# Attention scores as three products of split queries and keys, from one set of buffers

## The reference, cut to what matters

```python
q = (c_q @ w_uq).reshape(B, S, N_HEADS, QK_NOPE_DIM + QK_ROPE_DIM)
q_nope = q[..., :QK_NOPE_DIM]
q_rope = apply_rope(q[..., QK_NOPE_DIM:], cos[:, :, None, :], sin[:, :, None, :])
kv = (c_kv @ w_ukv).reshape(B, S, N_HEADS, QK_NOPE_DIM + V_HEAD_DIM)
k_nope, v = kv[..., :QK_NOPE_DIM], kv[..., QK_NOPE_DIM:]
for qs in range(0, S, Q_BLOCK):            # Q_BLOCK = 128
    qe = qs + Q_BLOCK
    s = (einsum('bqhd,bkhd->bhqk', q_nope[:, qs:qe], k_nope[:, :qe])
         + einsum('bqhr,bkr->bhqk', q_rope[:, qs:qe], k_rope[:, :qe])) * scale
    causal = arange(qe)[None, :] <= arange(qs, qe)[:, None]
    p = softmax(where(causal, s, -inf), axis=-1)
    outs.append(einsum('bqhk,bkhd->bqhd', p, v[:, :qe]))
```

## Time and profile before

| | us |
|---|---|
| median of 3 runs | 3156.41 (3155.97 to 3156.82) |
| the profiled execution | 3158.01, its span 3156.2 |
| PE busy over the whole span | 2728.8 (86%) |
| attention, from its first product to its last DVE write | 1432.2 to 1800.2 |

### The profile page before, as it was taken

One profiled execution on the slowest core, in us unless ns is written; L12 is line 12 of the kernel. 1 busy time (PEld: TensorE's weight loads), 2 busy tenths in 40 slices (PEclk: granted clock), 3 DMA queues, 4 the chain that ended last, 5 costly groups with the idle time before them and its releaser, 6 DMA issues. The chain is left out here.

```text
span 3156.2 us, 42227 instructions
## 1 busy us (share of the span) xinstructions
PE 2728.8 (86%) x16267; PEld 1769.1 (56%) x16269; DVE 1512.5 (48%) x2421; ACT 962.5 (30%) x1707; POOL 313.3 (10%) x378
## 2 busy tenths in 40 slices
PE   6999888979999999989999895897887758988785
PEld 3778687758888878755555583332322642333221
DVE  4248886577777757834555554111111760111114
ACT  6212275453333344434344321010110630110004
POOL 0000075000000000211011000111110000111100
PEclk9999999989999999999999996899999868999998
DMA  8511043122332266520000317999999669999996
GB/s 325 195 54 33 22 167 149 57 67 90 107 115 103 91 229 228 166 92 11 7 4 4 114 51 304 422 409 424 425 423 397 233 250 420 400 424 424 425 419 265
DMA packets 198828, 674.24 MB, mean 214 GB/s; under 512 B 42256, under 2 KB 83671, under 8 KB 144863
## 3 DMA queue, kind: packets, MB, share of 16 engines
q1 hardware_dynamic: 180192, 637.92, 51.8%
q0 software_dynamic: 18432, 33.60, 2.8%
HBM read 624.82 MB, written 80.15 MB: 223 GB/s over the span
## 5 line engine op out<-in xcount | busy, mean ns | idle before, releaser
L3335 PE MATMUL psum<-moe_ring,hreg 128*32 128x512 f32 x2832 | 481.5, 629 | 38.9 <-DMA moe_top<-in_moe_w 20.9
L3440 DVE TENSOR_TENSOR ex_hb<-ex_sil,psum 128x256 f32<-128x256 f32 x64 | 27.0, 421 | 567.4 <-ACT ex_sil L3413 567.4
L3335 PE MATMUL psum<-x,hreg 128*32 128x512 f32 x848 | 231.2, 662 | 56.4 <-DMA moe_ring<-in_moe_w 34.1
L3335 PEld LDWEIGHTS psum<-moe_ring,hreg 128*32 128x32 f32 x2832 | 140.9, 116 | 242.9 <-issue 197.1
L1507 PE MATMUL psum<-gu_hi,x1r 128*128 128x512 f32 x712 | 226.4, 394 | 9.4 <-DVE x1r L1634 5.1
L1860 PE MATMUL psum<-dn_op 128*128 128x512 f32 x924 | 211.7, 392 | 4.3 <-DVE dn_op L1955 4.3
L3387 PE MATMUL psum<-moe_ring,hreg 128*32 128x512 f32 x1216 | 196.8, 607 | 18.0 <-issue 10.9
L1860 PEld LDWEIGHTS psum<-dn_op 128*128 128x128 f32 x924 | 174.5, 189 | 41.5 <-DVE dn_op L1955 5.1
L3335 PE MATMUL psum<-moe_top,hreg 128*32 128x512 f32 x416 | 195.3, 625 | 0.0
L3413 ACT ACTIVATE ex_sil<-psum 128x256 f32<-128x256 f32 x64 | 24.5, 384 | 557.5 <-PE psum L3335 557.5
L1507 PE MATMUL psum<-gu_hi,gu_er 128*128 128x512 f32 x504 | 158.6, 389 | 0.0
(11 more groups left out here) (643 smaller groups left out, 5759.2 us busy)
## 6 DMA issues: line engine op xcount, KB each, us to landing
moe_ring<-in_moe_w SPq DMA_DIRECT2D x244, 1024.0 KB, 22.2
x<-in_moe_w SPq DMA_DIRECT2D x84, 1024.0 KB, 20.4
moe_top<-in_moe_w SPq DMA_DIRECT2D x48, 1024.0 KB, 26.7
x<-in_w_down SPq DMA_DIRECT2D x77, 256.0 KB, 2.9
x<-midrow SPq DMA_DIRECT2D x77, 256.0 KB, 3.5
XF<-in_w_ada SPq DMA_DIRECT2D x19, 1024.0 KB, 6.7
moe_ring<-yrow SPq DMA_DIRECT2D x16, 1024.0 KB, 11.3
xrow<-x SPq DMA_DIRECT2D x24, 512.0 KB, 3.7
```

The source lines that it names most:

```text
L3335: last = pe.matmul(ps[i][r, :], xT[i][:, k, r], place[HOME[n, j]][:, kk * 512:(kk + 1) * 512], start=k == 0, stop=k == KD - 1)
L3440: dve.tensor_tensor(hb[i][:, :], sil[q % 2][:, :], ps[i][:, DE:2 * DE], ALU.mult).then_inc(hbd, 1)
```

## The change

The scores are computed from queries and keys that are each split into a high part (rounded to fp32r) and a low part (the rest). Each float32 product becomes three fp32r products: high times high, high times low, low times high.

Queries go through one float32 buffer, `whole`, written by DVE from PSUM; ACT copies it to QH[w], DVE subtracts to get QL[w]. Keys of one head are copied by ACT from PSUM to KH[w], and DVE subtracts PSUM minus KH into KL[w]. The other head's keys wait in a float32 buffer, `second`, until their place is free; then ACT copies them to KH and DVE subtracts. There is one set of QH, QL, KH, KL, with a place for each head w, where QT and KT were there twice. So the order of items is by head: the head w = p % 2 first for t = 7 to 4, then the other head for t = 7 to 4 and 3 to 0, then the first again for t = 3 to 0. The k turn of pair p+1 stands behind item 11, the q turn of its first head behind item 12, the q turn of its second head behind item 0 of pair p+1 itself.

The core of the diff:

```diff
-PAIR_ITEMS = [(g, t, w) for g in (1, 0) for t in (4 * g + 3, 4 * g + 2, 4 * g + 1, 4 * g) for w in range(2)]
+def pair_items(p):
+    first = p % 2
+    return [(g, t, w) for g, heads in ((1, (first, 1 - first)), (0, (1 - first, first)))
+            for w in heads for t in (4 * g + 3, 4 * g + 2, 4 * g + 1, 4 * g)]
...
-            if p + 1 < HEAD_PAIRS and i in (8, 10, 12):
...
+            if p + 1 < HEAD_PAIRS and i == 11:
+                turns.append(("k", p + 1, 0))
+            if p + 1 < HEAD_PAIRS and i == 12:
+                turns.append(("q", p + 1, (p + 1) % 2))
+            if p > 0 and i == 0:
+                turns.append(("q", p, 1 - p % 2))
...
# PE
                     elif kind == "k":
                         pe.wait_ge(k_ev, p + 1)
+                        pe.wait_ge(k_lo, p + 1)
                     else:
-                        pe.wait_ge(q_ev, 2 * p + i + 1)
+                        pe.wait_ge(q_full, query_number(p, i) + 1)
...
+                    if i == 0:
+                        (waits for k_hi, k_lo, q_hi, q_lo of the first head)
+                    if i == 4:
+                        (waits for k2_hi, k2_lo, q_hi, q_lo of the second head)
...
                     if c:
-                        pe.matmul(S[:, 0:c], q, key[:, 0:c], start=True, stop=True)
-
-                    pe.matmul(S[:, c:e], q, key[:, c:e], start=True, stop=False)
+                        for x, y, z in ((QH, KH, 0), (QH, KL, 1), (QL, KH, 2)):
+                            pe.matmul(S[:, 0:c], x[w][:, rows], y[w][:, 0:c], start=z == 0, stop=z == 2)
+                    for x, y, z in ((QH, KH, 0), (QH, KL, 1), (QL, KH, 2)):
+                        pe.matmul(S[:, c:e], x[w][:, rows], y[w][:, c:e], start=z == 0, stop=False)
...
# ACT
+                    act.activation(KH[w][ROWS[w], :], bank(n)[ROWS[w], :], ACT.Identity, bias=0.0).then_inc(k_hi, 1)
+                    if p >= 1:
+                        act.wait_ge(k2_lo, p)
+                    act.activation(second[ROWS[1 - w], :], bank(n)[ROWS[1 - w], :], ACT.Identity, bias=0.0).then_inc(k_ev, 1)
+
+                def second_keys(n, p):
+                    w = 1 - p % 2
+                    act.wait_ge(item, n + 1)
+                    act.wait_ge(k_ev, p + 1)
+                    act.activation(KH[w][ROWS[w], :], second[ROWS[w], :], ACT.Identity, bias=0.0).then_inc(k2_hi, 1)
+
+                def queries(n, p, w):
+                    act.wait_ge(q_full, query_number(p, w) + 1)
+                    act.activation(QH[w][:, :], whole[:, :], ACT.Copy).then_inc(q_hi, 1)
...
+                for w in range(2):
+                    last = act.activation(KH[w][ROWS[1 - w], :], K.KT[0][w][ROWS[1 - w], :], ACT.Copy)
+                last.then_inc(rope_hi, 1)
...
# DVE
                 def queries(n, p, w):
                     dve.wait_ge(item, n + 1)
-                    dve.tensor_tensor(QT[p % 2][w][:, :], bank(n), K.CS[w][:, :], ALU.mult).then_inc(q_ev, 1)
+                    dve.wait_ge(q_lo, query_number(p, w))
+                    dve.tensor_tensor(whole[:, :], bank(n), K.CS[w][:, :], ALU.mult).then_inc(q_full, 1)
+
+                def low_queries(n, p, w):
+                    dve.wait_ge(q_hi, query_number(p, w) + 1)
+                    dve.tensor_tensor(QL[w][:, :], whole[:, :], QH[w][:, :].bitcast(F32), ALU.subtract).then_inc(q_lo, 1)
+                    if w != p % 2:
+                        dve.wait_ge(k2_hi, p + 1)
+                        dve.tensor_tensor(KL[w][ROWS[w], :], second[ROWS[w], :], KH[w][ROWS[w], :].bitcast(F32), ALU.subtract).then_inc(k2_lo, 1)
+
+                def low_keys(n, p):
+                    w = p % 2
+                    dve.wait_ge(item, n + 1)
+                    dve.wait_ge(k_hi, p + 1)
+                    dve.tensor_tensor(KL[w][ROWS[w], :], bank(n)[ROWS[w], :], KH[w][ROWS[w], :].bitcast(F32), ALU.subtract).then_inc(k_lo, 1)
...
+                    if kind == "k":
+                        low_keys(n, p)
+                    elif kind == "q":
+                        if split is not None:
+                            low_queries(*split)
                         queries(n, p, i)
+                        split = n, p, i
                     elif kind == "s":
+                        if split is not None and i == 0:
+                            low_queries(*split)
+                            split = None
                         row_max(n, p, i)
+                        if split is not None:
+                            low_queries(*split)
+                            split = None
                         if len(done) >= 2:
                             copy_turned(*done[-2])
```

More of the change, by code:

```diff
@@ L2344, in attention @@
         wq_hi, wq_lo, wk_hi, wk_lo = K.wq_hi, K.wq_lo, K.wk_hi, K.wk_lo
-        QT = [[sb(f"QT{s}{w}", [P, L]) for w in range(2)] for s in range(2)]
+        QH, QL = ([sb(f"{n}{w}", [P, L], F32R) for w in range(2)] for n in ("QH", "QL"))
+        KH, KL = K.KH, K.KL
+        whole, second = sb("whole", [P, L]), sb("second", [P, L])
         zero = sb("zero", [P, 2, 16])
@@ L2359, in high @@
         def high(m):
-            return sum(1 for n in range(m) if PAIR_ITEMS[n % NI][1] >= 4)
+            return sum(1 for n in range(m) if pair_items(0)[n % NI][1] >= 4)
         def turned(m):
@@ L2371, in _ @@
                     if p >= 2:
[L2372 removed]
+                        sp.wait_ge(item, last_query(p - 2) + 1)
                     load_query_weights(sp, K, A, p, w_in[p % 2])
[L2374 removed]
+                sp.wait_ge(item, last_query(HEAD_PAIRS - 1) + 1)
                 sp.dma_start(K.WO[:, :, :], A["mla_w_o_2"][0].rearrange("(k p) n -> p k n", p=P)).then_inc(K.wo_in, 16)
@@ L2385, in turned_rope @@
                     if p >= 2:
-                        pool.wait_ge(item, at["q", p - 2, 1] + 1)
+                        pool.wait_ge(item, last_query(p - 2) + 1)
                     split_query_weights(pool, K, p).then_inc(w_ok, 1)
@@ L2502, in keys @@
                 def keys(n, p):
+                    w = p % 2
                     act.wait_ge(item, n + 1)
[L2504 to L2509, removed]
+                    act.activation(KH[w][ROWS[w], :], bank(n)[ROWS[w], :], ACT.Identity, bias=0.0).then_inc(k_hi, 1)
[10 more added lines that the diff above has]
+                    act.activation(QH[w][:, :], whole[:, :], ACT.Copy).then_inc(q_hi, 1)
                 def weights(n, p, i):
-                    g, t, w = PAIR_ITEMS[i]
+                    g, t, w = pair_items(p)[i]
                     m = NI * p + i
@@ L2535, in _ @@
                         keys(n, p)
+                    elif kind == "q":
+                        queries(n, p, i)
+                        if i != p % 2:
+                            second_keys(n, p)
                     elif kind == "s":
@@ L2780, in mla @@
         K.CKV = sb("CKV", [P, L])
-        K.KT = [[sb(f"KT{s}{w}", [P, L]) for w in range(2)] for s in range(2)]
+        with nc.sbuf_tensor("mla_KTr", [P, 4, L], F32R) as under:
+            K.KL, K.KH = [under[:, w, :] for w in range(2)], [under[:, 2 + w, :] for w in range(2)]
+        rope_rows = sb("KT", [P, 4, L])
+        K.KT = [[rope_rows[:, w, :] for w in range(2)]]
         K.CS = [sb(f"CS{w}", [P, L]) for w in range(2)]
```

53 lines of the change are left out of this document (34 added, 19 removed).

## The result

The changed kernel takes 3203.41 us (median of 4 runs, 3203.02 to 3205.37), the kernel before 3156.61 us (4 runs, 3155.97 to 3158.48): a ratio of 1.0145, 95% interval 1.0133 to 1.0157. The forecast was 3175 us with a range to 3195. The direction was right, the size was not: +47 us instead of +18.

A forecast was written before the change was run, and what follows sets the result against it. The wide half was taken as bound by PE's work, the narrow half by the PE, DVE, ACT, PE round trip. 15.2 + 1.1 + 1.7 + 0.4 = +18.4 us gave 3175 us, range 3160 to 3195.

The forecast's parts named there:

- the seven steps: Seven apply-to-apply distances of the wide half in attention: 47.2 us each, 330.4 against 315.25, +15.2 us.
- the start: Start of the attention stage: first apply +1.1 us from added splits, and +1.7 us once for the clock.
- the tail: Last pair of the stage: no k and q turns, but late items wider than today, +0.4 us.
- one fall, at the start: PE's clock falls once, at 4.2 us of idle time ahead of the third item, costing +1.7 us.
- a fall in each pair as a rival: PE's clock falls to half in the narrow half of each pair: +12 us more, 3187; chance 0.15.
- The walk: Turn-by-turn layout of one pair from the wide half's apply: 47.2 us against 45.3, PE idle 8.9 against 4.8.
- the chain of row maximum, exponential and item: In the wide half this chain comes near PE's pace and leaves PE 0.5 us idle in all.
- The four longest waits: PE idle 1.35 us ahead of the q turn, 0.75 at item 14, 2.1 at item 12's transposes, 2.5 at narrow apply.
- the wait ahead of the q turn: PE waits for ACT's copies of the keys and DVE's subtraction before the q turn, 1.35 us idle.
- PE's gain: Three fp32r products replace each float32 score product: -2.2 us a pair of PE's work, bounds -2.9 to -1.0.
- the rival that PE's gain arrives: New waits hide behind work in attention, so 8 pairs gain 2.2 us each: 18 us faster, 3138; chance 0.07.
- The rival of a copy that overtakes the subtraction: One way PE's gain arrives: copies PE waits for overtake DVE's subtractions; 18 us faster, 3138; chance 0.07 for that rival.

The follow-up runs named there:

- experiment 2: The changed kernel with two float32 products nobody reads ahead of each of PE's two long waits; 3186.01 us, ratio 1.0087.
- experiment 7: The changed kernel with DVE's copies ahead of its subtractions, and POOL subtracting QL and the second head's KL for pairs 1 to 7; 3170.65 us, ratio 1.0038.
- experiment 5: The changed kernel with DVE's copy ahead of the queries' subtraction only at item 13, in the narrow half; 3189.40 us, ratio 1.0102.
- experiments 8: The kernel of experiment 7 with the first q turn one item later, behind item 13 in place of item 12; 3192.63 us, ratio 1.0111.
- 9: The changed kernel with both heads' keys copied out of PSUM at once into second, KH and KL made from it, and DVE's subtraction later; 3190.43 us, ratio 1.0103.
- experiment 1: The changed kernel with DVE's low_queries behind copy_turned in each item's turn, and behind the first row_max at the start; 3180.85 us, ratio 1.0075.
- 6: The changed kernel with low_queries and the second head's KL behind copy_turned only at item 1; 3190.06 us, ratio 1.0112.
- experiment 4: The kernel before with each float32 score product made as three fp32r products of rounded operands, no low parts, order kept; 3147.58 us, ratio 0.9970.
- experiment 3: The kernel before with only the new order of items and turns, float32 scores, two sets of buffers, no splits; 3154.18 us, ratio 0.9994.
- experiment 10: The kernel of experiment 7 with the keys' single copy out of PSUM and QL subtracted in two halves; 3151.57 us, ratio 0.9989.

## Why the prediction was wrong

The miss, in the profiled executions 3205.4 - 3176.4 = 29.0 us: 39.9 - 15.2 = 24.7 in the seven steps, 4.0 - 2.8 = 1.2 at the start, -0.3 in the tail, 3.4 behind the stage.

- **The clock was the step that failed.** The forecast has one fall, at the start, and gave a fall in each pair as a rival with a chance of 0.15. It falls 12 times in the seven steps. Holding it (experiment 2) takes 2.35 us off a pair, 16.5 of the 24.7 us. The size of one fall was near: 1.7 taken, 1.57 measured in experiment 7, 1.1 and 1.6 at the two places of a pair, 1.4 on average over the 12. What was wrong is the number of them and the chance. The walk itself held what was needed: 0.75 and 2.1 us of idle time close together ahead of the transposes, 2.5 ahead of apply, and a clock that falls in the tail of the kernel before where PE works as thinly. How often it would fall the walk could not say: experiments 5 and 7 have the same waits with and without a fall. With the 16.5 us that the 12 falls cost, the sum would have been 3191 us. The rival also looked at one place only and left the wait ahead of apply out.
- **The remaining 8.3 us are in the walk**, 1.2 us a pair at full clock. Part is the wide half: the walk let it lose 0.5 us to the chain of row maximum, exponential and item, and it takes 0.5 longer than that. The other part arises late in the narrow half. Timeline of PE in experiment 2, behind apply at 1561.21, items 12 and 0:

```profile
1570.90 0.73 PE L2475 MATMUL psum<-mla_KTr,at_QH 128*128 128x512 f32 x2
...
1582.16 0.72 PE L2473 MATMUL psum<-mla_KTr,at_QH 128*128 128x512 f32 x2
```

  Item 12 starts after 9.69 us (walk 9.8), so the wait of 0.52 ahead of it costs nothing that the walk hadn't in another place. Item 0 starts after 20.95 (20.6), and apply of the narrow half after 30.65 (30.1). What makes the wide half longer was not taken apart.
- **The four longest waits and their places were right**, all within 0.2 us in the pair shown, and so was what ends them. That the wait ahead of the q turn is the hold on the PSUM place was shown by experiments 8 and 9, that the two long ones are the subtraction ahead of the copy by 1, 5 and 6.
- **PE's gain** was forecast as 2.2 us a pair in PE's work. Timeline of PE in the changed kernel, a chunk of 128 columns, and an item whose first chunk of 512 stands behind transposes:

```profile
1604.03 0.33 PE L2475 MATMUL psum<-mla_KTr,at_QH 128*128 128x128 f32 x2
1604.20 0.27 PE L2475 MATMUL psum<-mla_KTr,at_QL 128*128 128x128 f32 x1
1604.32 0.23 PE L2476 MATMUL psum<-at_mask 128*128 128x128 bf16 x1
...
1609.37 0.72 PE L2473 MATMUL psum<-mla_KTr,at_QH 128*128 128x512 f32 x2
...
1610.17 0.40 PE L2475 MATMUL psum<-mla_KTr,at_QH 128*128 128x256 f32 x2
```

  Three products of 128 columns take 1604.32 - 1604.03 = 0.29 us; the forecast had 0.36, and float32 0.22. By that price the gain would be 2.5 us a pair. But three products of 512 columns behind transposes take 1610.17 - 1609.37 = 0.80 us and not 0.69; part of it comes back, since seven transposes ahead of them take 0.70 us instead of 0.77. What is measured for a whole pair is 1.8 us less busy time (experiment 4). Of it 1.2 a pair arrives even where nothing else is changed, so the rival that PE's gain arrives, 18 us, was priced twice too high: 9.4 us was to be had without the low parts. The Trainium skill ("FP8 and Floating Point Precision", section TensorE Precision Notes) counts a float32 product as four passes; worked out from that, an estimate for three is 0.165 us at 128 columns. The trace agrees roughly at 512 columns (0.69 to 0.86, four fifths), and not at 128, where the measured 0.29 is dearer than one float32 product.
- **The start** was +1.1 and +1.7 for the clock, and came out at +4.0. The third item starts at 1449.27 (forecast 1448.4) behind 4.02 us of idle time (4.2), and the clock falls there as forecast.
- **The order** was costed at nothing, and experiment 3 shows no cost. The single set of buffers was never tried alone, so its share isn't known.
- **The rival of a copy that overtakes the subtraction** (experiment 1) was right about the cause and wrong about the gain: 3181 instead of 3138. DVE still has the same 4.9 us of subtractions in the same narrow half, and whatever is put behind them is late. Only when most of them left DVE and each wait for a place was shortened (experiment 10, which joins 7 and 9) did a step fall under 45 us.

A rule of the Trainium skill fits this in kind: "TensorE: Matmul & The Clock Gate", section HAM oscillation, describes a loop whose recurring wait makes each round start at the low clock. The trace agrees in part: 12 falls in seven steps, with waits of about 2 us for DVE instead of waits for a DMA, but in experiments 5 and 7 the same wait brings a fall in one round and none in others.

## What to carry to other kernels

Where a walk gives new waits in a loop on PE, price the case that the clock falls at each of them in each round (1.1 to 1.6 us apiece here) and give it a real chance before the sum is made. Here falls came at waits from 0.84 to 2.55 us and also stayed out at them, so the number of falls has to be a range. Filling the waits with products that nobody reads was worth 17 us. On an engine with strict order put the short operation that PE waits for ahead of the long one that it doesn't, then look at what stands behind the long one: it moves the loss (half of it here). Giving most of the long ones to an idle engine took another 10 us (experiment 7). A PSUM place that is held for a subtraction can be freed by one plain copy to SBUF.

## What the runs showed of the hardware

- A clock fall can come well after PE has resumed: PE restarts at 1598.03 behind its wait, and by the shares of the windows the clock falls at about 1599.1. So its cost shows as longer work, not as idle time, and a list of waits doesn't hold it.
- Waits of equal length (2.55 us in experiment 5, 0.84 in experiment 7) bring a fall in one pair and none in another. Most falls last 3.4 us, some 6.8 (experiment 5 from 1629.1).
- An fp32r product of 128 columns costs about 0.10 us, hardly less than one of 256 columns (0.12): three of them are dearer than one float32 product at 128 columns (0.29 against 0.22) and cheaper from 256 on (0.36 against 0.43). Behind float32 transposes three of 512 columns take 0.80 us instead of 0.69.
- POOL subtracts 128 rows of 1024 columns in 2.35 us, DVE in 1.23, and 64 rows take each of them as long (2.38 and 1.21).
